# A fused mixer and expert trunk: norm sums of one pre-added tile, splits ahead of stage rests, first expert unit high part first, output in quarters

## What is computed

```python
for layer in range(DEPTH):
    h = rmsnorm(x, norm1_g[layer])
    proj = h @ w_in[layer]
    ...
    merged = (gates[:, :, 0] * (y_a @ w_br_a[layer]).astype(F32)
              + gates[:, :, 1] * (y_b @ w_br_b[layer]).astype(F32)
              + gates[:, :, 2] * (y_c @ w_br_c[layer]).astype(F32)
              + gates[:, :, 3] * (y_d @ w_br_d[layer]).astype(F32))
    x = x + merged.astype(x.dtype) @ w_out[layer]
    h2 = rmsnorm(x, norm2_g[layer])
    if layer % 2 == 0:
        f = swiglu(h2, ffn_wg[idx], ffn_wu[idx], ffn_wd[idx])
    else:
        f = moe_ffn(h2, router_w[idx], moe_wg[idx], moe_wu[idx], moe_wd[idx])
    x = x + f
return rmsnorm(x, final_g)
```

## Time and profile before

| | us |
|---|---|
| median of 3 runs | 1858.77 |
| the three runs | 1862.35, 1858.38, 1858.77 |
| the profiled execution | 1860.32 |
| its span, first to last instruction | 1858.5 |
| TensorE busy | 1838.1 (99%) |
| VectorE busy | 1483.2 (80%) |
| ScalarE busy | 1192.8 (64%) |
| GpSimd busy | 193.7 (10%) |

### The profile page before, as it was taken

How to read it: one execution, slowest core, us unless ns; L and a number is a source line. 1 busy time by engine, 2 the same in 40 slices (tenths; PEclk the granted TensorE clock), 3 DMA queues, 4 the chain that set the end, 5 groups by cost and what they waited for, 6 DMA issues and landing times.

```text
span 1858.5 us, 27339 instructions
## 1 busy us (share of the span) xinstructions
PE 1838.1 (99%) x10331; PEld 1595.2 (86%) x10331; DVE 1483.2 (80%) x1308; ACT 1192.8 (64%) x1010; POOL 193.7 (10%) x147
## 2 busy tenths in 40 slices
PE   9999999999999999999999999999999999999997
PEld 8998878999999998779788888888888888888876
DVE  7776677755578866776988988888899898988887
ACT  5655654533346546555767777777777777877775
POOL 1055000000010460000840000000000000000010
PEclk9999999999999999999999999999999999999999
DMA  9454455455454444446799999999999999999994
GB/s 355 173 182 159 160 180 176 165 184 188 174 200 164 154 179 169 172 160 237 303 375 372 385 389 377 367 373 393 384 377 375 369 394 378 373 375 381 385 393 174
DMA packets 74545, 521.27 MB, mean 280 GB/s; under 512 B 8176, under 2 KB 8432, under 8 KB 13680
## 3 DMA queue, kind: packets, MB, share of 16 engines
q1 hardware_dynamic: 71568, 509.34, 72.7%
q0 software_dynamic: 2912, 11.01, 1.6%
HBM read 509.83 MB, written 10.49 MB: 280 GB/s over the span
## 4 chain that ended last, share of the span: by engine, by line
PE 94%; DVE 2%; DMA 2%; ACT 1%; issue 1%; SPq 0%; DVEq 0%; ACTq 0%
PE psum L1445 92%; PE psum L1892 1%; DMA weight_raw<-mix_w 1%; DMA weight_raw<-moe_w 1%; DVE proj L1021 0%; PE psum L1820 0%; DVE yb_lo L748 0%; DVE weight_raw_r L789 0%; DVE yb_lo L755 0%; PE psum L1528 0%; PE psum L1652 0%; DVE proj L771 0%; DVE weight_lo L1035 0%; DVE weight_lo L745 0%; ACT proj L717 0%
## 5 line engine op out<-in xcount | busy, mean ns | idle before, releaser
L745 DVE TENSOR_TENSOR weight_lo<-weight_raw,weight_hi 128x2048 fp32r<-128x2048 f32 x139 | 329.3, 2370 | 151.8 <-ACT weight_hi L416 150.8
L416 ACT ACTIVATE weight_hi<-weight_raw 128x2048 fp32r<-128x2048 f32 x139 | 265.2, 1910 | 144.2 <-PE psum L1445 140.4
L1445 PE MATMUL psum<-weight_lo,y_hi 128*128 128x512 f32 x768 | 304.3, 396 | 0.0
L1445 PE MATMUL psum<-weight_hi,y_hi 128*128 128x512 f32 x768 | 301.2, 392 | 2.4 <-DVE y_lo L748 1.8
L1445 PE MATMUL psum<-weight_hi,y_lo 128*128 128x512 f32 x768 | 299.8, 390 | 0.0
L1445 PE MATMUL psum<-weight_lo,y_lo 128*128 128x512 f32 x672 | 262.5, 391 | 0.0
L1445 PE MATMUL psum<-weight_raw_r,y_hi 128*128 128x512 f32 x576 | 224.9, 390 | 0.0
L1445 PE MATMUL psum<-proj_r,y_hi 128*128 128x512 f32 x576 | 224.4, 390 | 0.0
L1445 PE MATMUL psum<-h_hi,weight_hi 128*128 128x256 f32 x704 | 201.1, 286 | 0.0
L1445 PE MATMUL psum<-h_lo,weight_hi 128*128 128x256 f32 x704 | 199.2, 283 | 0.0
L1445 PE MATMUL psum<-h_hi,weight_lo 128*128 128x256 f32 x704 | 199.2, 283 | 0.0
(11 more groups left out here) (315 smaller groups left out, 3802.0 us busy)
## 6 DMA issues: line engine op xcount, KB each, us to landing
proj<-moe_w SPq DMA_DIRECT2D x144, 1024.0 KB, 6.9
weight_raw<-moe_w SPq DMA_DIRECT2D x144, 1024.0 KB, 6.8
weight_raw<-mix_w SPq DMA_DIRECT2D x106, 1024.0 KB, 4.8
first_raw<-moe_w SPq DMA_DIRECT2D x48, 1024.0 KB, 7.0
weight_raw<-ff_w SPq DMA_DIRECT2D x33, 1024.0 KB, 4.8
made_rows<-zeros POOLq DMA_DIRECT2D x1, 4096.0 KB, 22.1
made_rows<-pool_tmp SPq DMA_DIRECT2D x8, 512.0 KB, 6.4
weight_raw<-mix_w SPq DMA_DIRECT2D x4, 512.0 KB, 8.4
```

What stands on the lines that cost most here:

```text
L416: A(hi[:, slot, :], raw[:, slot, :], ACT.Copy).then_inc(hi_done, 1)
L745: V.tensor_tensor(lo[:, slot, :], raw[:, slot, :], hi[:, slot, :].bitcast(f32), ALU.subtract).then_inc(lo_done, 1)
L1445: return nc.tensor.matmul(o, a, b_, start=start, stop=stop, skip_group_check=True, **k)
```

## The change

Eight edits, in the order of the program:

1. The load of the first parameters is issued behind the first half of x instead of ahead of it.
2. Norm sums: GpSimd adds all three further pairs onto pair 0 and then its second tile onto its first (four additions instead of two); TensorE multiplies one tile by ones instead of four.
3. VectorE: in `pool_out` and `short` the split of unit u + 2 comes ahead of the wait for ScalarE's high part and the rest. What it does for `y_norm` is the same: the split of unit 47 comes ahead of the whole stage. ScalarE's high part of unit 47 comes ahead of its share of `y_norm` too.
4. End of the dense SwiGLU: the low part of pair 2 comes ahead of the addition of pair 3.
5. First expert item, VectorE: the hidden chunk 0 is multiplied ahead of the split of unit 6.
6. First expert item, TensorE: units 0 and 1 first multiply with the high part of the gathered rows (8 matmuls), then wait for the low part (4 matmuls).
7. ScalarE and VectorE scale the output in column halves, with a semaphore step each.
8. SyncE stores four quarters of 256 KB instead of two halves.

```diff
-            sp.dma_start(par[:, :PAR_FIRST], par_in[0, :, :PAR_FIRST]).then_inc(par_loaded, 16)
             for u in range(2):
                 for part in range(2):
                     if u == 0:
                         sp.dma_start(x[:, 4 * part:4 * part + 4, :], x_in[:, 4 * part:4 * part + 4, :]).then_inc(x_loaded[part], 16)
+                    if u == part == 0:
+                        sp.dma_start(par[:, :PAR_FIRST], par_in[0, :, :PAR_FIRST]).then_inc(par_loaded, 16)
...
-            for t in range(TT):
-                sp.wait_ge(*((S["tok_std"], 2 * TT + 1), (S["rstd_done"], 3))[t])
-                sp.dma_start(out[:, t, :], x_gain[:, t, :]).then_inc(stored, 16)
+            for n in range(2):
+                for t in range(TT):
+                    sp.wait_ge(*((S["tok_std"], 2 * TT + 1 + n), (S["rstd_done"], 3 + n))[t])
+                    sp.dma_start(out[:, t, cols(n)], x_gain[:, t, cols(n)]).then_inc(stored, 16)
...
-            A(x_gain[:, 0, :], x_gain[:, 0, :], ACT.Copy, scale=rstd[:, 0, :]).then_inc(S["tok_std"], 1)
+            for n in range(2):
+                A(x_gain[:, 0, cols(n)], x_gain[:, 0, cols(n)], ACT.Copy, scale=rstd[:, 0, :]).then_inc(S["tok_std"], 1)
...
+                if behind_split:
+                    stage(behind_split, layer)
...
                 for name, n in PLAN:
-                    stage(name, layer)
-                    for _ in range(n):
-                        mixer_unit(layer, u)
+                    behind = {"pool_out": "pool_low", "short": "short"}.get(name)
+                    if behind != name and name != "y_norm":
+                        stage(name, layer)
+                    for m in range(n):
+                        mixer_unit(layer, u, behind if m == 0 else None)
                         u += 1
-                for u in range(u, MIX_UNITS):
-                    mixer_unit(layer, u)
+                for m in range(u, MIX_UNITS):
+                    mixer_unit(layer, m, "y_norm" if m == u else None)
...
+                        if q == PAIRS - 1:
+                            low(2, q - 1)
                         added(q)
-                        if q:
+                        if 0 < q < PAIRS - 1:
                             low(2, q - 1)
...
-            for v in (4, 5, 6):
-                split_e(v)
+            split_e(4)
+            split_e(5)
             dve.wait_ge(unit_used, RING + MOE_U + 4)
             gated(0, 0)
+            split_e(6)
             split_e(7)
...
-                for q in (1, 2):
+                for q in range(1, PAIRS):
                     gp.wait_ge(S["sq_done"], PAIRS * n + q + 1)
-                    last = G.tensor_tensor(flat(sq[:, 0:2, :]), flat(sq[:, 0:2, :]), flat(sq[:, 2 * q:2 * q + 2, :]), ALU.add)
-                    if q == 1:
-                        link(last)
-                last.then_inc(S["sq_added"], 1)
+                    link(G.tensor_tensor(flat(sq[:, 0:2, :]), flat(sq[:, 0:2, :]), flat(sq[:, 2 * q:2 * q + 2, :]), ALU.add))
+                G.tensor_tensor(sq[:, 0, :], sq[:, 0, :], sq[:, 1, :], ALU.add).then_inc(S["sq_added"], 1)
...
-                for k in (0, 1, KT - 2, KT - 1):
-                    if k == 0:
-                        pe.wait_ge(S["sq_added"], n + 1)
-                    elif k == KT - 2:
-                        pe.wait_ge(S["sq_done"], PAIRS * (n + 1))
-                    last = mm(bank(7)[:, 0:SEQ], C_("ones"), sq[:, k, :], k == 0, k == KT - 1)
-                last.then_inc(S["norm_sum"], 1)
+                pe.wait_ge(S["sq_added"], n + 1)
+                mm(bank(7)[:, 0:SEQ], C_("ones"), sq[:, 0, :], True, True).then_inc(S["norm_sum"], 1)
...
+            def first_up(half):
+
+                split_e_is(half, 0)
+                pe.wait_ge(S["eg_hi_done"], half + 1)
+                for k in range(4):
+                    w, kk = slice(k * CHUNK_F, (k + 1) * CHUNK_F), 4 * half + k
+                    mm(bank(4), xg_hi[:, kk, :], hi_e(half)[:, w], kk == 0, False)
+                    mm(bank(4), xg_hi[:, kk, :], lo_e(half)[:, w], False, False)
+                pe.wait_ge(S["eg_lo_done"], half + 1)
+                for k in range(4):
+                    kk = 4 * half + k
+                    last = mm(bank(4), xg_lo[:, kk, :], hi_e(half)[:, k * CHUNK_F:(k + 1) * CHUNK_F], False, kk == KT - 1)
+                last.then_inc(unit_used, 1)
...
-            for v in range(4):
-                if v < 2:
-                    pe.wait_ge(S["eg_lo_done"], v + 1)
-                if v == 2:
-                    pe.wait_ge(S["x_tok_done"], 2 * TT)
-                up(bank(4 + v // 2), v, v % 2)
+            first_up(0)
+            first_up(1)
+            pe.wait_ge(S["x_tok_done"], 2 * TT)
+            up(bank(5), 2, 0)
+            up(bank(5), 3, 1)
```

More of the change, by code:

```diff
@@ L400, in _ @@
                 load_e(expert * ITEM_UNITS + v, v, last_item * ITEM_UNITS + v - RAW_E)
-            for t in range(TT):
-                sp.wait_ge(*((S["tok_std"], 2 * TT + 1), (S["rstd_done"], 3))[t])
-                sp.dma_start(out[:, t, :], x_gain[:, t, :]).then_inc(stored, 16)
-            sp.wait_ge(stored, 16 * TT)
+            for n in range(2):
+                for t in range(TT):
+                    sp.wait_ge(*((S["tok_std"], 2 * TT + 1 + n), (S["rstd_done"], 3 + n))[t])
+                    sp.dma_start(out[:, t, cols(n)], x_gain[:, t, cols(n)]).then_inc(stored, 16)
+            sp.wait_ge(stored, 16 * 2 * TT)
         @block.scalar
@@ L591, in _ @@
                 for name, n in PLAN:
-                    behind = name.startswith("conv") or name in ("var", "spatial", "pool_out", "short")
+                    behind = name.startswith("conv") or name in ("var", "spatial", "pool_out", "short", "y_norm")
                     if not behind:
@@ L793, in merged_low, with mixer_unit @@
                 rest(flat(h_lo[:, 2 * q:2 * q + 2, :]), bank(4 + q), flat(h_hi[:, 2 * q:2 * q + 2, :]), S["m_lo"])
-            def mixer_unit(layer, u):
+            def mixer_unit(layer, u, behind_split=None):
                 b = base_of(layer)
@@ L954, in stage @@
                     last.then_inc(S["yd_f"], 1)
+                elif kind == "pool_low":
                     dve.wait_ge(S["yd_hi"], layer + 1)
@@ L1311, in _ @@
             dve.wait_ge(S["end_gain"], 2 * TT)
-            V.tensor_scalar(x_gain[:, 1, :], x_gain[:, 1, :], rstd[:, 1, :], None, ALU.mult).then_inc(S["rstd_done"], 1)
+            for n in range(2):
+                V.tensor_scalar(x_gain[:, 1, cols(n)], x_gain[:, 1, cols(n)], rstd[:, 1, :], None, ALU.mult).then_inc(S["rstd_done"], 1)
         @block.gpsimd
```

## The result

| | before | changed |
|---|---|---|
| median, us | 1858.77 (7 runs, 1857.50 to 1862.35) | 1863.98 (7 runs, 1862.77 to 1865.75) |
| ratio, 95% interval | 1 | 1.0026 (1.0017 to 1.0036) |
| span of the profiled execution | 1858.5 | 1862.1 |
| TensorE busy | 1838.1 | 1835.8 |

A forecast was written before the change was run, and what follows sets the result against it. The prediction took TensorE, busy 99% of the span, to bound the kernel. Its terms summed to +3.2 us without the clock and +5.95 with it, so 1858.77 became 1864.7 us, range 1858.5 to 1868.0.

The forecast's parts named there:

- The bound and the places: TensorE, busy 99% of the span, bounds the kernel; only its own work and the places where it stands still count.
- The norm of y_b: Unit 47's split, now ahead of the norm, delays it and stalls TensorE before unit 46: +2.6 us per layer, +5.2 in all.
- Rival 2: Unit 47's split hides in VectorE's idle time before the norm; unit 44's ring place speaks against it; 1854.6 us, chance 0.1.
- The end of the dense SwiGLU: Pair 3 is added 1.8 us later, VectorE's split of unit 88 waits for GpSimd's addition, TensorE starts late: +1.36 us.
- Norm sums in layer 1: TensorE's work shrinks by 1.29 us, but the last rest of h holds the next matmul: -0.74 us.
- The short convolution: The rest behind a split in `short` ends later than TensorE needs it: +0.3 us per layer, +0.6 in all.
- First expert item: High part first brings 0, as unit 4's split doesn't move; hidden chunk first starts the first down unit earlier: -1.45 us.
- Rival 4: First expert edits differ: unit 6's split arrives late instead, 1866.2 us, or TensorE keeps all of 2.1, 1864.0; chance 0.07.
- The end: Output in quarters: first store issued some 0.55 us sooner, four issues taking 1.66; net -0.5 us.
- The clock: Half-clock stretches behind the two y_b stalls cost 1.4 us each, +2.8; the median's executions taken as without such stretches.
- rival 1: Stalls stay, clock falls behind neither (1862.0 us, chance 0.2) or only one (1863.4 us, chance 0.15).
- Rival 3: Experts are bound by DMA, so the 1.45 us gained ahead of them is given back: 1866.2 us, chance 0.1.

The follow-up runs named there:

- experiment 5: Changed kernel with the norm of y_b put back ahead of the split of unit 47 on VectorE alone; median 1856.63 us.
- experiment 1: Changed kernel with the norm of y_b put back ahead of the split of unit 47 on VectorE and ScalarE; median 1856.51 us, ratio 0.9985.
- experiment 2: Kernel before with one move alone, the split of unit 47 ahead of the norm of y_b on both engines; median 1867.98 us, ratio 1.0046.
- experiment 7: Changed kernel with the norm sums as before (four products, two additions); median 1865.27 us.
- experiment 4: Changed kernel with the norm of y_b, the short convolution's rest and the end of the dense SwiGLU in the old order; median 1855.09 us, ratio 0.9979.
- experiment 8: Kernel before with only the first hidden chunk multiplied ahead of the split of unit 6; median 1857.11 us, ratio 0.9988.
- experiment 10: Kernel before with only the norm sums of one pre-added tile; median 1856.92 us, ratio 0.9986.
- experiment 12: Kernel before with only the output scaled in column halves and stored in four quarters; median 1858.89 us, ratio 0.9997.
- experiment 6: Changed kernel with pair 3 added ahead of the low part of pair 2 again at the end of the dense SwiGLU; median 1861.74 us.
- experiment 11: Kernel before with only units 0 and 1 of the first expert item multiplying first with the high part; median 1859.19 us, ratio 1.0000.
- experiment 3: Changed kernel with twelve matmuls of ones ahead of TensorE's wait for the rests of y_b, in both layers; median 1861.15 us.

## Why the prediction held, point by point

TensorE's way through the program is compared between the same matmuls in the two profiled executions; each term is the change of one such distance.

| term | forecast | measured |
|---|---|---|
| start and layer 0's norm sums | 0 | -0.06 |
| short convolution's rest, two layers | +0.6 | +0.8 |
| norm of y_b, two stalls | +5.2 | +5.0 |
| norm sums in the dense SwiGLU, and unit 88 | +0.07 | -0.12 |
| norm sums in layer 1 | -0.74 | -0.64 |
| high part first in the expert item | 0 | -0.02 |
| hidden chunk first | -1.45 | -1.29 |
| output in quarters | -0.5 | -0.28 |
| sum without clock | +3.2 | +3.4 |
| half-clock stretches (+1.6, -1.6), the last item's wait (+0.3), small shifts in the experts | (clock: +2.8) | +0.2 |
| difference of the spans | | +3.6 |

- *The bound and the places.* Right: every term is a wait of TensorE or work of its own. Beside the terms only the clock and the last item's wait showed.
- *The norm of y_b.* Right in mechanism, place and size: 2.48 us in each layer where 2.6 were forecast, and experiment 5 puts it on VectorE's order. Experiments 1 and 2 show it from both sides. Rival 2 (the split hides in the idle time) fell on the ring place, as the text said: ScalarE had the high part at 294.28, 2.0 us behind unit 44's last matmul.
- *The end of the dense SwiGLU.* Unit 88 was forecast at +1.36 and came at +1.16, with the norm sums at the forecast -1.29 (between unit 46 of layer 0 and the additions). The mechanism is the forecast's: the split of unit 88 began at 544.87 while GpSimd's addition ran (544.71 to 546.12), and ended 2.15 us behind that addition's end; I had taken 2.28 to 2.55 for that part, which is the missing 0.2. GpSimd's next addition, half as large, took 2.67 us and ended 0.6 us behind the split. Each waited out the other. The Trainium skill (SBUF — State Buffer, section "Who interferes with whom") says that the two engines share a port pair, which only one of them can have at a time; the traces agree, with 3.40 us for the split in the changed kernel against the 2.28 of experiment 7, and with GpSimd's 6.18 us in experiment 4. The forecast took it that GpSimd's addition, begun first, goes ahead of the split; that came true here, and not in experiment 4.
- *Norm sums in layer 1.* Right: the wait of 0.40 for h_lo turned up as said.
- *The short convolution.* Slightly low. Unit 26 came 0.3 us later in each layer, as forecast, but the matmul behind a wait takes 0.31 us to the next in place of 0.23, which with what follows adds 0.1 in each layer. The forecast leaves out this restart behind every new wait.
- *First expert item.* Right, with the split of unit 4 as what sets unit 4. TensorE waits 0.73 us at the first down unit, for the rest of the chunk. Rival 4 fell with it: it wanted 0 or -2.1 where -1.29 came.
- *The end.* The sign was right, the size was half. The forecast of -0.5 had the first store issued 0.55 us sooner and four issues in 1.66, which puts the last issue 0.28 later, and so left 0.78 for the shorter transfer. The first issue came 0.42 us sooner (0.95 us behind the reciprocal's start instead of 1.37) and the four took 1.82 us, so the last was issued 0.53 later (2.31 us behind the reciprocal's start instead of 1.78). It landed 2.7 us behind its issue, against 3.5 for the last store before: 0.8 less, as the sum needed. The issues were mis-sized, not the transfer. The medians over the stores were 2.5 us for 256 KB and 3.1 for 512:

```profile
out<-proj SPq DMA_DIRECT2D x4, 256.0 KB, 2.5
```

  The Trainium skill (DMA: Bandwidth & Descriptors, section "Anatomy of one DMA — SWDGE (gpsimd) path") has about 2.0 us fixed for a DMA on GpSimd's path. These stores are SyncE's, and the first of each kernel, with no other store ahead of it, took 2.6 us for 512 KB and 2.0 for 256 KB; a straight line through the two meets no bytes at 1.4 us, so the traces here don't bear the page's figure out. The prediction's -0.55 by that page doesn't follow either: the section's variable part gives 0.6 us for 256 KB, and with the last issue 0.28 later an estimate by it is -0.3.
- *The clock.* Forecast +2.8, a chance of 0.38 for both stalls costing clock and 0.15 for one. The medians leave 5.2 - 3.4 = 1.8 us to it beyond what the kernel before loses too. Filling the stalls removed 2.8. So the size was right within what can be told, but two things in the term weren't. It had a fixed loss behind each stall, while the clock fell behind five of eight such stalls, and in the changed kernel's profiled execution behind one. And it took the median runs of the kernel before as free of such stretches, while five of the eight profiled executions with the norm in its old order held one (the kernel before, experiments 4, 8, 10 and 12). The profiled execution is rival 1's case with one loss, 1863.4; the median of 1863.98 lies between it and the forecast's 1864.7 and can't tell them apart. That it came so near to the forecast is in part luck, with the terms without clock 0.2 too low and the clock's 1.0 too high.
- *Rival 3* (the experts bound by DMA). Fell: experiments 1, 4, 8 and 10 keep their gains in the medians, and the stretch from 905 to 1780 us has almost no gap in the changed kernel either (PE busy 873.91 of 875).

## What to carry to other kernels

Moving an instruction into another engine's idle time needs more than room: ask when its own operands come, and what stands behind it in that engine's order. A split that fits the idle time by length, but whose operand arrives at the idle time's end, pushes everything behind it by its full length (here 2.48 us for a split of 2.28). And where a stall of some us can't be avoided on TensorE, matmuls of no use in it may give back part of what it costs. But taking the stall away gave 7.5 us, filling it 2.8.

## What the runs showed of the hardware

**The same stall can cost clock or not.** In the four profiled kernels with full stalls of 2.76 us (the changed one, experiments 2, 6 and 7) eight stalls stood, and five had a half-clock stretch of 3.4 us behind them. Experiment 7 (first two rows, in the columns of the earlier trace rows) had one behind both stalls, experiment 6 (last two) behind neither:

```profile
302.50:305.90 3.40, 3.40 (x9) 2.65 (x8) 1.08 (x1) 2.28 (x2) 0.00 (x0) 0.50 0.02 5
835.00:838.40 3.40, 3.01 (x7) 2.46 (x8) 0.43 (x2) 3.16 (x4) 0.00 (x0) 0.50 0.00 0
...
302.30:305.70 3.40, 3.40 (x15) 2.84 (x16) 0.60 (x1) 2.77 (x3) 0.00 (x0) 1.00 0.02 5
831.40:834.80 3.40, 3.40 (x15) 2.84 (x16) 0.57 (x1) 2.80 (x3) 0.00 (x0) 1.00 0.00 0
```

In the eight kernels with 0.3 us of wait there (the kernel before, experiments 1, 4, 5, 8, 10, 11, 12), none of sixteen had one, and of the four filled or half-filled places none. Elsewhere it was as uneven. The hidden chunk's wait of 2.0 us was followed by one in experiments 2 and 10, and not in the kernel before and experiments 11 and 12. The last item's wait was followed by one at 1.78 us in the kernel before and at 1.96 in experiment 4, and not at 2.10 in the changed kernel nor at 1.66 to 1.88 in experiments 5, 6, 8 and 12. Shorter waits weren't safe either: 0.60 us in experiment 8, and the end of the dense SwiGLU in experiments 2 and 12, where waits of 0.46 and 1.05 us stand close together. Within these runs it looks like a chance at each stall; what decides it isn't shown. Each stretch costs about 1.6 us: from layer 1's unit 46 to the head of the expert stage (matmuls at 887.58 and 881.02) it was 54.68 us in the changed kernel, with the stretch, and 53.11 before, without.

**A part of the spread between runs of one kernel goes with this clock.** Of the 25 runs of the kernel before beside the first four experiments, the seven with a mean granted clock of 0.999 lie between 1857.81 and 1859.14 us, and the one with 0.996 at 1861.23. Beside the last four it is looser: one run with 0.998 took 1863.34 us, and one with 0.946 took 1861.04. So the mean clock of a run doesn't give its time.

**A wait near the last expert item varies by itself.** TensorE's wait for the last hidden chunk of the loop (1.78 us before) was 0.3 to 2.1 us over the fourteen profiles, with no plain relation to how early TensorE came there: 1.96 in experiment 4, the earliest, and 0.30 in experiment 3. ScalarE waits there for weights to land. This blurs every comparison of single executions by a us or more. What sets it was not followed up.

**Not tried:** the parameters' place and the pooling rest's by themselves; both are inside the -0.06 and the +0.8 of the table, and no wait of TensorE's names them.
